# One weight part's home cleared of small router tiles, and a new order in the first units of mixer B

## The chip, the cores and the metric

The kernel runs on one core of one Trainium2 chip. The metric is the device time of one launch in microseconds, the median of several runs. All arrays are float32.

## What is computed

One layer of an encoder block over a sequence of 512 tokens of width 1024. Mixer B and the mixture of experts are the parts that matter here:

```python
def dilated_window_attention(q, k, v):            # mixer B: 12 heads in 3 groups (window, dilation)
    ...
            s = jnp.einsum('bqhd,bqkhd->bhqk', qb, kg).astype(jnp.float32)
            s = s - slopes[gi][:, None, None] * jnp.abs(jnp.asarray(off, jnp.float32))[None, None, :]
            s = jnp.where(valid[None, None], s, NEG_INF)
            lse = jax.nn.logsumexp(s, axis=-1)
            p = jnp.exp(s - lse[..., None]).astype(vg.dtype)
            outs.append(jnp.einsum('bhqk,bqkhd->bqhd', p, vg))
...
def expert_choice_swiglu(h, w_router, w_gate, w_up, w_down):
    aff = jax.nn.softmax(jnp.einsum('bsd,de->bse', h, w_router).astype(jnp.float32), axis=-1)
    g, idx = lax.top_k(jnp.swapaxes(aff, 1, 2), cap)          # 16 experts, 64 tokens each
    xin = jax.vmap(lambda hb, ib: hb[ib])(h, idx)
    a = jnp.einsum('becd,edf->becf', xin, w_gate)
    u = jnp.einsum('becd,edf->becf', xin, w_up)
    y = jnp.einsum('becf,efd->becd', jax.nn.silu(a) * u, w_down) * g[..., None].astype(h.dtype)
    ...
x = x + (gate_a * mixerA(h) @ w_o_a + gate_b * mixerB(h) @ w_o_b) @ w_out
x = x + expert_choice_swiglu(rms_norm(x, norm2_g), w_router, w_gate, w_up, w_down)
```

## The kernel before

Every engine has one program written out by hand, and semaphores tie the five together. Nothing is scheduled by a tool: what stands first in an engine's program is issued first, and an instruction that waits holds all that stands behind it on its engine.

The program has these stages: the projections of mixer A (from 0 us), the attention of mixer A in 32 units (`u` 0 to 31), mixer B, the gates and branch projections, the output projection (`res_steps`) with the router woven in, the selection of tokens, and then the experts in 8 pairs (`gate_up`, `down`, `scatter`).

**Mixer B.** Units 32 to 39 are the first half (`hp` 0, four token tiles for each of two heads) and 40 to 47 the second (`hp` 1). `NA` is 32. A unit goes round three engines:

- TensorE writes the scores (`scores_b`). It does so two units ahead: in unit `u` it issues the scores of `u + 2`, which must wait until VectorE has finished the maximum of unit `u` (`nmax_done`).
- VectorE adds the distances of the two dilated groups to a part of `dist` (line 2052), then makes biased scores and their maximum (line 2058, 768 columns).
- ScalarE takes the exponential (line 889), VectorE the reciprocal and the product with it (`norm_probs`, lines 1985 and 1987, semaphore `probs_normed`).
- TensorE transposes the result with six matmuls (`turn_probs`, lines 1352 and 1357), and ScalarE copies it out (`read_probs`).

The dilated distances are the same for every token tile, but the kernel overwrites the place in `dist` where they lie, so VectorE first copies them to `far` (line 2033).

Between these steps TensorE has projections to do that depend on nothing in mixer B: `fill` issues as many of their steps (three matmuls of 512 columns each, lines 1169 to 1171) as the plan `B_FILL` gives a unit. It is `([2, 3, 4, 5, 7, 8, 8, 8], [3, 6, 7, 8, 11, 14, 16, 16])`, counted up: two steps in unit 32, three in unit 40, and three in unit 41. The first fill of either half needs the output of the heads before to be read out of its PSUM bank (`low_o`, line 1991, semaphore `o_lo_done`).

**The expert weights.** They come in 192 parts of 1 MB, into 20 homes. SyncE issues all loads in the order of the parts, but for a few at the start. Until TensorE begins with the experts, 20 parts are loaded, each as soon as the tensors that used its home before are dead; each later part waits until TensorE has used the part that its home holds (`w_slot_used`). Part 17 goes to the second half of `wslot7`, 24 to 32 KB behind `W0`. Before, three small tiles of the router lay in that place (`w_rt_wide`, `four_parts`, `four_sum`), so SyncE waited for the third router result, `logits_done`, ahead of it:

```python
            load_part(15)
            sp.wait_ge(logits_done, 3)
            load_part(17)
            sp.wait_ge(sumsq2, 2)
            sp.wait_ge(x2_turned, 2)
            sp.wait_ge(xn_lo_done, 4)
            load_part(18)
            sp.wait_ge(proj_done, len(groups))
            for m in (7, 11, 12, 16):
                load_part(m)
```

**The squares of the second norm.** ScalarE squares each token tile for its sum (`square_x2`, line 1016); the squares themselves are thrown away, into `squares2`. GpSimd makes the reciprocal root of the sum, which VectorE needs for the logits. `high_xn` writes the high part of tile `c` to `xn`.

Of the kernel before, what the change touches and what calls it, by code (L numbers as in the profile page):

```python
# [28 lines left out]
ACT = mybir.ActivationFunctionType  # L29
# [5 lines left out]
P = 128  # L35
SEQ = 512
D = 1024
NT = SEQ // P
# [8 lines left out]
NE = 16  # L47
# [37 lines left out]
def encoder_block(nc, x, norm1_g, w_in, b_gates, q_norm_g, k_norm_g, w_o_a, w_o_b, w_out, norm2_g,  # L85
# [13 lines left out]
    def sb(name, shape, kib, dt=F32):  # L99
        return nc.alloc_sbuf_tensor_at(name, [P] + shape, dt, offset=base + int(kib * KIB))  # L100
# [48 lines left out]
    out_hi = sb("out_hi", [HALF_OUT, KC, P], W0, F32R)  # L149
    out_lo = sb("out_lo", [HALF_OUT, KC, P], W0 + 16, F32R)  # L150

    squares2 = sb("squares2", [D], 105.5)
    h2T = sb("h2T", [2, KC, P], 96)
    LANES = 32 + NE
    aff_wide = sb("aff_wide", [NT, 32], 111)
# [3 lines left out]
    slot_id = sb("slot_id", [CAP], 110)  # L159
    logit = sb("logit", [NT, NE], 110.25)  # L160
    w_rt = sb("w_rt", [KC, NE], 110.5)
    w_rt_wide = sb("w_rt_wide", [KC, 32], W0 + 28)
    four_parts = sb("four_parts", [2, P], W0 + 29)
    four_sum = sb("four_sum", [NE], W0 + 30)
    best = sb("best", [CAP], 101)
    left = sb("left", [2, SEQ // 2], 98)
    other = sb("other", [CAP], 100)
# [57 lines left out]
    with ExitStack() as ctx:  # L225
        def sem(name):
# [9 lines left out]

        turned_two = [psum[:, 4 + 2 * i:6 + 2 * i, :].rearrange("p b (k i) -> p (b k) i", i=P)
                      for i in range(2)]
        g1_wide = psum[:, 2:4, :].rearrange("p b n -> p (b n)")
        pp = bank[0:4]  # L240
        tp = bank[4:8]
# [167 lines left out]
        def tile_summed(eng, c, p=None):  # L409

            if p is None:
                p = 2 if c == NT - 1 else 1
            eng.wait_ge(proj_read_dve, N_COL + g_at[("res", p, c)] - RES0 + 1)
# [159 lines left out]
        def _(sp):  # L573
# [102 lines left out]
            load_part(13)  # L676
            load_part(14)
            load_part(15)
            sp.wait_ge(logits_done, 3)
            load_part(17)  # L680
            sp.wait_ge(sumsq2, 2)
            sp.wait_ge(x2_turned, 2)
# [91 lines left out]
        def _(act_):  # L774
# [236 lines left out]
            def square_x2(n, c, p, cols, into):  # L1011

                tile_summed(act_, c, p)
                if n:
                    act_.wait_ge(sumsq2, n)
                act_.activation(squares2[:, cols], x2[:, c, cols], ACT.Square, accum_out=into).then_inc(sumsq2, 1)

            def square_tile(c):
                square_x2(c, c, None, slice(0, D), ssq[:, c:c + 1])
# [21 lines left out]

            def high_xn(c):
                tile_summed(act_, c)
                act_.activation(xn_hi[:, c, :].rearrange("p (h k i) -> p h k i", h=2, k=HALF),
                                x2[:, c, :].rearrange("p (h i k) -> p h k i", h=2, k=HALF), ACT.Copy)\
                    .then_inc(xn_hi_done, 1)
# [118 lines left out]
        def _(pe):  # L1165
# [240 lines left out]
            for hp in range(2):  # L1406
                todo = [(g, at[g[1:]]) for g in col_groups[N_COL_A:N_COL_A + 1]] if hp == 0 else \
                    [(("gate", 0, 0), at[("ga", 0)]), (("gate", 0, 1), at[("gb", 0)])]
                first, end = NA + 2 * NT * hp, NA + 2 * NT * (hp + 1)
                first_behind = (col_groups[N_COL_A + 1], at[col_groups[N_COL_A + 1][1:]])  # L1410
                scores_b(first)
                if hp == 0:
                    values_a(OA - 1)
                    pe.wait_ge(proj_read_dve, N_COL_A)
                scores_b(first + 1)
                for u in range(first, end):
                    if u + 2 < end:
                        scores_b(u + 2)
                    if u == first:

                        pe.wait_ge(o_lo_done, OA + hp)
                    fill(B_FILL[hp], u - first, todo)
                    if u >= end - 2:
                        pe.wait_ge(nmax_done, end - 1)
                    if hp == 0 and u == end - 2:
                        col_steps(*first_behind, 0, 3)
                    if u == end - 1:
                        if hp == 0:
                            col_steps(*first_behind, 3, KC)
                        else:  # L1430
                            col_steps(("gate", 1, 0), at[("ga", 1)], 0, KC // 2)
                    turn_probs(u)
                pe.wait_ge(nmax_done, end)
                if hp == 0:
                    for g in col_groups[3 * NG:]:
                        col_group(g, at[g[1:]])

                    pe.wait_ge(proj_read_dve, 2 * NG + 2)
                    values_b(0)
                    pe.wait_ge(proj_read_dve, 4 * NG)  # L1440
                else:
                    col_steps(("gate", 1, 0), at[("ga", 1)], KC // 2, KC)
                    pe.wait_ge(proj_read_act, N_TOK + 2)
                    values_b(1)
                    col_group(("gate", 1, 1), at[("gb", 1)])
# [106 lines left out]
            pe.wait_ge(aff_done, 2)  # L1552
            turn_aff(0)

            keep_clock(4)
            pe.wait_ge(aff_done, NT)
            turn_aff(1).then_inc(route_turned, 1)

# [301 lines left out]
        def _(dve):  # L1860
# [169 lines left out]
                    low_o(O_LOW.index(u))  # L2030

            dve.wait_ge(dist_in, 16)
            settle(dve.tensor_copy(far[:, :], dist[:, 0, SEQ:SEQ + 2 * P]))
            for hp in range(2):
                first, end = NA + 2 * NT * hp, NA + 2 * NT * (hp + 1)
                if hp:
# [4 lines left out]
                for u in range(first, end + 2):  # L2041
# [4 lines left out]
                    if u < end:  # L2046
                        head, c = divmod(u - NA, NT)

                        dve.wait_ge(score_done, NA + 2 * (u - NA) + 1)
                        dve.tensor_tensor(dist[:, c, SEQ:SEQ + 2 * P],
                                          far_two[u % 2][:, 1, :, :].rearrange("p g n -> p (g n)"), far[:, :],
                                          ALU.add).then_inc(far_added, 1)
                        dve.wait_ge(far_added, u - NA + 1)
                        dve.wait_ge(score_done, NA + 2 * (u - NA) + 2)
# [396 lines left out]
```

## Time and profile before

| | us |
|---|---|
| median of 3 runs | 862.12 |
| lowest and highest | 861.91, 864.86 |
| the profiled execution | 861.86 |
| its span, first to last instruction | 859.8 |
| TensorE busy | 839.4 |
| VectorE busy | 379.3 |
| ScalarE busy | 264.1 |

The span is 2.06 us shorter than the time of the same execution; that is what lies around it. In the rows further down, PE is TensorE's matmuls, PEld its weight loads, DVE VectorE, ACT ScalarE, POOL GpSimd, and SPq the queue in which SyncE issues loads. A matmul's duration overlaps that of the next, so TensorE's pace is read from start to start.

### The profile page before, as it was taken

How to read it: one execution, taken by the hardware profiler on the slowest of the kernel's cores; microseconds unless marked ns; L12 is line 12 of the kernel's file. 1: busy time of each engine (PE TensorE's matmuls, PEld its weight loads, DVE VectorE, ACT ScalarE, POOL GpSimd, SP SyncE). 2: the span in 40 equal slices, each digit the busy share in tenths (PEclk: the TensorE clock that was granted, in tenths of full speed). 3: DMA queues.
4: the chain of work that ended last, by engine and by line, in shares of the span. 5: the costliest groups of instructions: out<-in, count | busy, mean ns of one | idle time of the engine just before them, and what ended most of it. 6: DMA issues, size and time to landing. Idle time of an engine off the chain costs nothing.

```text
span 859.8 us, 10399 instructions
## 1 busy us (share of the span) xinstructions
PE 839.4 (98%) x4197; PEld 513.2 (60%) x4197; DVE 379.3 (44%) x665; ACT 264.1 (31%) x461; POOL 29.0 (3%) x50
## 2 busy tenths in 40 slices
PE   9999999999999999999999999999999998989996
PEld 8898866687878888888534343344433433334343
DVE  6377987797715254427322237223131321321351
ACT  6333876695624233216011010010100101001231
POOL 1050000000000000003000000000000000000010
PEclk9999999999999999999999999999999999999999
DMA  9830112023034234884899999999999999999996
GB/s 285 179 98 2 50 50 98 25 76 109 20 123 143 84 107 144 311 356 180 331 410 425 429 428 426 429 428 427 428 428 427 426 430 428 426 423 429 427 420 265
DMA packets 81490, 239.19 MB, mean 278 GB/s; under 512 B 8102, under 2 KB 63526, under 8 KB 65828
## 3 DMA queue, kind: packets, MB, share of 16 engines
q1 hardware_dynamic: 76016, 235.94, 69.7%
q10 hardware_dynamic: 5284, 2.09, 1.0%
q8 instruction: 33, 0.54, 0.3%
q0 software_dynamic: 144, 0.51, 0.1%
q14 instruction: 13, 0.11, 0.0%
HBM read 235.92 MB, written 2.62 MB: 277 GB/s over the span
## 4 chain that ended last, share of the span: by engine, by line
PE 88%; DMA 8%; DVE 1%; ACT 1%; issue 1%; POOLq 0%; POOL 0%; SPq 0%; DVEq 0%; ACTq 0%
PE psum L1657 21%; PE psum L1169 11%; PE psum L1689 11%; PE psum L1171 11%; PE psum L1170 11%; DMA wslot<-in_w_down 7%; PE psum L1614 3%; PE psum L1708 3%; PE psum L1357 2%; PE psum L1818 2%; PE psum L1326 2%; PE psum L1369 1%; PE psum L1669 1%; PE psum L1175 1%; PE psum L1622 1%; PE psum L1379 1%
## 5 line engine op out<-in xcount | busy, mean ns | idle before, releaser
L1657 PE MATMUL psum<-wslot,xinT 128*64 128x512 f32 x1000 | 221.9, 595 | 3.7 <-DMA wslot<-in_w_up 1.9
L1657 PEld LDWEIGHTS psum<-wslot,xinT 128*64 128x64 f32 x1000 | 69.5, 137 | 141.3 <-issue 131.8
L1689 PE MATMUL psum<-wslot,actT 128*64 128x512 f32 x424 | 95.8, 596 | 4.5 <-DMA wslot<-in_w_down 4.5
L1169 PE MATMUL psum<-hT_hi,w_hi 128*128 128x512 f32 x208 | 82.4, 396 | 0.9 <-DVE oT_lo L1991 0.9
L1170 PE MATMUL psum<-hT_lo,w_hi 128*128 128x512 f32 x208 | 81.2, 390 | 0.0
L1171 PE MATMUL psum<-hT_hi,w_lo 128*128 128x512 f32 x208 | 81.2, 390 | 0.0
L1892 DVE TENSOR_TENSOR w_lo<-w_raw,w_hi 128x1024 fp32r<-128x1024 f32 (+1 forms) x46 | 52.9, 1174 | 44.4 <-ACT w_hi L805 44.3
L1689 PEld LDWEIGHTS psum<-wslot,actT 128*64 128x64 f32 x424 | 29.4, 137 | 60.4 <-issue 58.0
L1101 ACT ACTIVATE actT<-psum 128x512 f32<-128x512 f32 x16 | 9.6, 597 | 171.2 <-PE psum L1669 171.2
L2305 DVE TENSOR_TENSOR x<-x,psum 128x512 f32<-128x512 f32 x48 | 29.7, 681 | 57.0 <-PE psum L1708 57.0
L2295 DVE TENSOR_TENSOR y_lo<-psum,y_hi 64x512 fp32r<-64x512 f32 x28 | 19.3, 689 | 80.4 <-ACT y_hi L1111 80.0
L805 ACT ACTIVATE w_hi<-w_raw 128x1024 fp32r<-128x1024 f32 (+1 forms) x46 | 45.2, 1017 | 16.3 <-PE psum L1171 16.3
L1169 PEld LDWEIGHTS psum<-hT_hi,w_hi 128*128 128x128 f32 x208 | 39.0, 188 | 12.1 <-issue 2.8
L1171 PEld LDWEIGHTS psum<-hT_hi,w_lo 128*128 128x128 f32 x208 | 39.1, 188 | 8.4
L1170 PEld LDWEIGHTS psum<-hT_lo,w_hi 128*128 128x128 f32 x208 | 39.1, 188 | 7.8
L1096 ACT ACTIVATE act<-psum,slot_vals 128x512 f32<-128x512 f32 x16 | 11.0, 687 | 93.2 <-PE psum L1657 93.2
L2282 DVE SCALAR_TENSOR_TENSOR act<-psum,slot_vals,act 128x512 f32<-128x512 f32 x16 | 12.0, 750 | 59.1 <-ACT act L1096 59.0
L901 ACT ACTIVATE pT<-psum 128x512 f32<-128x512 f32 x48 | 28.5, 596 | 19.6 <-PE psum L1357 10.1
L1111 ACT ACTIVATE y_hi<-psum 64x512 fp32r<-64x512 f32 x28 | 16.5, 590 | 57.3 <-PE psum L1689 57.0
L1614 PE MATMUL psum<-xn,pick 128*128 128x512 f32 x120 | 29.4, 396 | 0.0
L2248 DVE TENSOR_TENSOR xinT<-psum,small 128x512 f32<-128x512 f32 x15 | 9.7, 686 | 40.0 <-PE psum L1622 40.0
L2288 DVE SCALAR_TENSOR_TENSOR act<-act,slot_fac,psum 128x512 f32<-128x512 f32 x16 | 12.0, 747 | 30.8 <-PE psum L1657 30.8
(285 smaller groups left out, 1306.5 us busy)
## 6 DMA issues: line engine op xcount, KB each, us to landing
wslot<-in_w_up SPq DMA_DIRECT2D x24, 2048.0 KB, 25.0
wslot<-in_w_gate SPq DMA_DIRECT2D x24, 2048.0 KB, 23.9
wslot<-in_w_down SPq DMA_DIRECT2D x22, 2048.0 KB, 22.4
w_raw<-in_w_in SPq DMA_DIRECT2D x34, 512.0 KB, 4.7
wslot<-in_w_up SPq DMA_DIRECT2D x15, 1024.0 KB, 11.0
wslot<-in_w_down SPq DMA_DIRECT2D x15, 1024.0 KB, 27.5
wslot<-in_w_gate SPq DMA_DIRECT2D x14, 1024.0 KB, 11.2
w_raw<-in_w_out SPq DMA_DIRECT2D x8, 512.0 KB, 4.9
```

The source lines that it names most:

```text
L805: act_.activation(hi, raw, ACT.Copy).then_inc(w_hi_done, 1)
L901: last = act_.activation(pT[:, head % 2, :, cols], tp[(0, 3)[u % 2]][:, :].rearrange("p (k i) -> p k i", i=P), ACT.Copy)
L1169: pe.matmul(out_, s_hi, m_hi, start=(k == 0), stop=False)
L1170: pe.matmul(out_, s_hi, m_lo, start=False, stop=False)
L1171: return pe.matmul(out_, s_lo, m_hi, start=False, stop=(k == n_k - 1))
L1614: mm = pe.matmul(bank[6 + f][:, :], pick[:, c, :, :], part[:, c, cols], start=(c == 0 and part is xn_hi), stop=(c == NT - 1 and part is xn ...
L1657: mm = pe.matmul(bank[2 * e + n][CAP * f:CAP * f + CAP, :], xinT[:, HALF * h + k, CAP * e:CAP * e + CAP], wslot[place_of(m)][:, k % PART, ...
L1689: mm = pe.matmul(bank[4 + e][CAP * f:CAP * f + CAP, :], actT[:, e, k, CAP * h:CAP * h + CAP], wslot[place_of(m)][:, k % PART, SEQ * f:SEQ ...
L1708: mm = pe.matmul(bank[added_bank(c, f)][:, :], give[:, p % 2, P * c:P * c + P], part[:, SEQ * f:SEQ * f + SEQ], start=(part is y_hi), stop ...
L1892: dve.tensor_tensor(lo, raw, hi.bitcast(F32), ALU.subtract).then_inc(w_split, 1)
L2295: dve.tensor_tensor(y_lo[rows, cols], bank[4 + e][CAP * f:CAP * f + CAP, :], y_hi[rows, cols].bitcast(F32), ALU.subtract).then_inc(y_lo_do ...
L2305: dve.tensor_tensor(part, part, bank[added_bank(c, f)][:, :], ALU.add).then_inc(added, 1)
```

## The change

1. `w_rt_wide`, `four_parts` and `four_sum` move to the 4 KB at 105.5 KB where `squares2` was. The squares of tiles 0 to 2 go to the place of tile `c` in `xn`, those of tile 3 to two PSUM banks (4 and 5). So `high_xn` waits for the squares of its tile, and the last squares wait for VectorE to have read tile 2 out of those banks. Four idle matmuls of `keep_clock` write to bank 1 instead of 5.
2. SyncE no longer waits for `logits_done` ahead of part 17.
3. In unit 32 VectorE adds the dilated distances from the last tile's place in `dist`, which is still whole until unit 35, and the copy to `far` comes in unit 33.
4. In the first unit of either half (32 and 40), TensorE's `turn_probs` stands ahead of the wait for `o_lo_done` and ahead of the fill.

```diff
-    squares2 = sb("squares2", [D], 105.5)
+    squares_by_tile = [sb(f"squares_by_tile{c}", [D], W0 + 64 + 8 * c) for c in range(NT - 1)]
-    w_rt_wide = sb("w_rt_wide", [KC, 32], W0 + 28)
-    four_parts = sb("four_parts", [2, P], W0 + 29)
-    four_sum = sb("four_sum", [NE], W0 + 30)
+    w_rt_wide = sb("w_rt_wide", [KC, 32], 105.5)
+    four_parts = sb("four_parts", [2, P], 106.5)
+    four_sum = sb("four_sum", [NE], 107.5)
+        last_squares = psum[:, 4:6, :].rearrange("p b n -> p (b n)")
             load_part(15)
-            sp.wait_ge(logits_done, 3)
             load_part(17)
-                act_.activation(squares2[:, cols], x2[:, c, cols], ACT.Square, accum_out=into).then_inc(sumsq2, 1)
+                if c < NT - 1:
+                    squares = squares_by_tile[c]
+                else:
+                    act_.wait_ge(h2T_dve_done, NT - 1)
+                    squares = last_squares
+                act_.activation(squares[:, cols], x2[:, c, cols], ACT.Square, accum_out=into).then_inc(sumsq2, 1)
             def high_xn(c):
                 tile_summed(act_, c)
+                act_.wait_ge(sumsq2, c + 1 + (c == NT - 1))
                     if u == first:
 
+                        turn_probs(u)
                         pe.wait_ge(o_lo_done, OA + hp)
                     fill(B_FILL[hp], u - first, todo)
...
-                    turn_probs(u)
+                    if u > first:
+                        turn_probs(u)
-            keep_clock(4)
+            keep_clock(4, bank[1])
             dve.wait_ge(dist_in, 16)
-            settle(dve.tensor_copy(far[:, :], dist[:, 0, SEQ:SEQ + 2 * P]))
+                        if u == NA + 1:
+                            settle(dve.tensor_copy(far[:, :], dist[:, NT - 1, SEQ:SEQ + 2 * P]))
                         dve.wait_ge(score_done, NA + 2 * (u - NA) + 1)
                         dve.tensor_tensor(dist[:, c, SEQ:SEQ + 2 * P],
-                                          far_two[u % 2][:, 1, :, :].rearrange("p g n -> p (g n)"), far[:, :],
+                                          far_two[u % 2][:, 1, :, :].rearrange("p g n -> p (g n)"),
+                                          dist[:, NT - 1, SEQ:SEQ + 2 * P] if u < NA + NT - 1 else far[:, :],
                                           ALU.add).then_inc(far_added, 1)
```

TensorE's order in unit 40, the first of the second half, before the change. The first rows are the scores of unit 42, then come three fill steps, the transposes of unit 40 (`probs_b_73`) and the scores of unit 43:

```order
L1338 MATMUL psum<-kB,oT_hi 128x2x128 [waits nmax_done]
L1338 MATMUL psum<-kB,qB 128x2x128
L1342 MATMUL psum<-kB,qB_next 128x512 x2
L1169 MATMUL psum<-hT_hi,w_hi 128x512 [waits proj_read_dve,w_split,o_lo_done]
L1170 MATMUL psum<-hT_lo,w_hi 128x512
L1171 MATMUL psum<-hT_hi,w_lo 128x512
...
L1352 MATMUL psum<-ident,probs_b_73 128x128 [waits pT_done,probs_normed]
L1352 MATMUL psum<-ident,probs_b_73 128x128
L1357 MATMUL psum<-ident,probs_b_73 128x128 x4
L1338 MATMUL psum<-kB,oT_hi 128x2x128 [waits nmax_done]
```

The same place in the changed kernel (its line numbers are 6 higher):

```order
L1344 MATMUL psum<-kB,oT_hi 128x2x128 [waits nmax_done]
L1344 MATMUL psum<-kB,qB 128x2x128
L1348 MATMUL psum<-kB,qB_next 128x512 x2
L1358 MATMUL psum<-ident,probs_b_73 128x128 [waits pT_done,probs_normed]
L1358 MATMUL psum<-ident,probs_b_73 128x128
L1363 MATMUL psum<-ident,probs_b_73 128x128 x4
L1175 MATMUL psum<-hT_hi,w_hi 128x512 [waits proj_read_dve,w_split,o_lo_done]
L1176 MATMUL psum<-hT_lo,w_hi 128x512
L1177 MATMUL psum<-hT_hi,w_lo 128x512
...
L1344 MATMUL psum<-kB,oT_hi 128x2x128 [waits nmax_done]
```

The six transposes with their wait for `probs_normed` moved ahead of nine fill matmuls in unit 40. In unit 32 they moved ahead of six in the same way.

## Rows read from the trace of the kernel before

**Rows 1.** The chain of work that ended last, shares of the span by engine.
```profile
PE 88%; DMA 8%; DVE 1%; ACT 1%; issue 1%; POOLq 0%; POOL 0%; SPq 0%; DVEq 0%; ACTq 0%
```

**Rows 2.** TensorE's waits (total, times, longest), and its last one in the timeline.
```profile
PE psum L1689 <- DMA wslot<-in_w_down: 4.5, 3, 1.9
...
774.58 7.09 PE L1689 MATMUL psum<-wslot,actT 128*64 128x512 f32 x32 [1.94 <-DMA wslot<-in_w_down]
```

**Rows 3.** Windows from 383.5 us on: busy times, granted clock, DMA share, GB/s.
```profile
383.50:397.50 14.00, 14.00 (x120) 11.94 (x118) 8.08 (x16) 11.95 (x18) 1.49 (x4) 1.00 0.02 7
...
416.60:420.60 4.00, 4.00 (x20) 1.37 (x22) 0.78 (x4) 0.00 (x0) 0.19 (x1) 1.00 0.38 84
420.00:440.00 20.00, 20.00 (x94) 7.47 (x92) 3.00 (x8) 2.57 (x3) 0.00 (x0) 1.00 0.99 373
440.00:690.00 250.00, 250.00 (x1185) 105.35 (x1183) 78.30 (x129) 29.40 (x49) 0.00 (x0) 1.00 1.01 427
690.00:850.00 160.00, 152.18 (x694) 64.39 (x690) 42.44 (x68) 24.66 (x39) 2.97 (x8) 1.00 1.01 425
```

**Rows 4.** SyncE's queue: three issues in its timeline, and its wait for the router.
```profile
371.13 0.91 SPq L632 DMA_DIRECT2D wslot<-in_w_up  x2
...
397.61 0.33 SPq L632 DMA_DIRECT2D wslot<-in_w_down  x1
...
418.48 8.93 SPq L632 DMA_DIRECT2D wslot<-in_w_down  x4
...
SPq L632 <- PE psum L1516: 25.6, 1, 25.6
```

**Rows 5.** Timeline of TensorE, units 40 and 41 of mixer B.
```profile
213.80 0.39 PE L1338 MATMUL psum<-kB,oT_hi 128*128 128x256 f32 x1 [0.45 <-DVE small L2058]
...
214.62 0.39 PE L1169 MATMUL psum<-hT_hi,w_hi 128*128 128x512 f32 x1
...
216.70 0.38 PE L1352 MATMUL psum<-ident,probs_b 128*128 128x128 f32 x2
...
217.27 0.36 PE L1338 MATMUL psum<-kB,oT_hi 128*128 128x256 f32 x1
```

**Rows 6.** Timeline of VectorE in the same units.
```profile
213.66 0.08 DVE L2058 DVE_READ_ACCUMULATOR2_ANT small<- 128x1 f32 x1
...
215.79 0.62 DVE L1987 TENSOR_SCALAR probs_b<-probs_b,small 128x768 f32<-128x768 f32 x1
```

**Rows 7.** Windows from unit 40 to the output projection.
```profile
214.40:231.00 16.60, 16.60 (x94) 14.06 (x93) 14.59 (x35) 11.69 (x26) 0.00 (x0) 1.00 0.11 33
231.00:381.00 150.00, 150.00 (x696) 122.55 (x695) 56.18 (x73) 47.30 (x64) 0.75 (x2) 1.00 0.51 174
```

**Rows 8.** Timeline of VectorE and TensorE, units 32 and 33.
```profile
165.70 0.29 DVE L2033 COPY far<-dist 128x256 f32<-128x256 f32 x1
...
166.03 0.42 DVE L2052 TENSOR_TENSOR dist<-psum,far 128x256 f32<-128x256 f32 x1
...
168.75 0.62 DVE L1987 TENSOR_SCALAR probs_b<-probs_b,small 128x768 f32<-128x768 f32 x1
169.28 0.68 DVE L1991 TENSOR_TENSOR oT_lo<-psum,oT_hi 128x512 fp32r<-128x512 f32 x1
...
170.02 0.51 PE L1169 MATMUL psum<-hT_hi,w_hi 128*128 128x512 f32 x1 [0.93 <-DVE oT_lo L1991]
...
172.74 0.62 DVE L1987 TENSOR_SCALAR probs_b<-probs_b,small 128x768 f32<-128x768 f32 x1
...
173.57 0.38 PE L1352 MATMUL psum<-ident,probs_b 128*128 128x128 f32 x2
```

**Rows 9.** Timeline around the last logits: ScalarE, GpSimd and VectorE.
```profile
399.24 0.42 ACT L1016 ACTIVATE squares<-x 128x256 f32<-128x256 f32 x1 [1.44 <-DVE x L2116]
...
400.44 0.55 POOL L719 TENSOR_TENSOR small<-small 128x1 f32<-128x1 f32 x1
...
401.10 0.29 DVE L2133 TENSOR_SCALAR logit<-psum,small 128x16 f32<-128x16 f32 x1
```

## The prediction, written before the changed kernel ran

> **What bounds the kernel now.** I began with the chain of work that ended last. TensorE holds 88% of it and DMA 8% [rows 1], so the question is which of the two sets the end. TensorE's waits answer it for the expert stage: only late there does it wait for weights, and the last of these waits ends at 774.58 us, after 1.94 us of idling [rows 2]. From there to the end the chain is TensorE's again.
>
> The windows of that stage show how it came to this. From 440 us on the loads run at 427 and 425 GB/s without a break [rows 3], and TensorE is a little faster than they are: it eats up the store of loaded parts until about 690 us and then waits. So the end is set by the moment at which the stream of loads becomes unbroken, plus its bytes at that rate. What sets that moment? Between 416.6 and 420.6 us the stream moves 84 GB/s, from 420 to 440 it moves 373 [rows 3]. All 20 homes are full there, and the next load goes out at 418.48 us [rows 4], when TensorE has used its first part. The stream therefore hangs on the moment when TensorE begins with the experts, and that on all that TensorE does before. The reader is to see a chain in two links: TensorE up to about 418 us, and a stream that TensorE itself starts.
>
> Ahead of the experts TensorE has almost no slack. From 214.4 to 231 us it is busy 16.60 of 16.60 us, and from 231 to 381 us 150.00 of 150 [rows 7]. A delay put in before that travels to the end whole.
>
> **Part 17 earlier: 0 us.** Before, its load leaves at 397.61 us, after a wait of 25.6 us for the router [rows 4]. After, it stands right behind part 15, whose issue is the second of the two at 371.13 us [rows 4], and it falls into a stretch in which the queues are idle (7 GB/s from 383.5 to 397.5 us, rows 3). One part is 1.049 MB, at 427 GB/s 2.46 us. But what is saved is not needed: the queue had already run dry by 416.6 us with this load in its old place, and the next home falls free only when TensorE has worked through a part. The 2.46 us become a longer pause ahead of 418.48 us. The parts read first have arrived in both kernels, since TensorE waits for none of them there: in all, its waits for loads come after 690 us. Bounds: 0, and a gain of 2.46 us if I misread the pause. I take 0.
>
> The Trainium skill (DMA: Bandwidth & Descriptors, section Where 436 GB/s comes from) gives 435 GB/s as the ceiling of the 16 engines together, and the 427 of the trace agree that the stream cannot be hurried. By that reading alone, a megabyte moved into an idle stretch would be worth its 2.4 us, an estimate from that page; it is rival 1 below.
>
> **Squares and router tiles: 0 us.** `high_xn` now waits for squares that stand ahead of it on ScalarE, so the wait is met. The wait of the last squares is for a copy that stands, in VectorE's program, ahead of the residual add for which these squares wait anyway. What no row shows is ScalarE writing squares to PSUM. The cover is thin in one place: the 256-column square starts at 399.24 us and takes 0.42, GpSimd's root runs from 400.44 for 0.55 to 400.99, and VectorE's step that needs it begins at 401.10 [rows 9]. So a square that is 0.1 us slower is hidden, and one that is 0.2 slower costs 0.1. I bound it by half and double the 0.42 us: it gains nothing (VectorE's own maximum stands just ahead of that step), or costs up to 0.3. The nearest row is the same instruction with its old target; 0 is my value.
>
> **The copy to `far`: 0 us by itself.** Its step is 0.33 us (165.70 to 166.03, rows 8). It leaves the way to the first exponential, so that the add, the maximum, the exponential and the product of unit 32 all come 0.33 us sooner: the product begins at 168.42 instead of 168.75, and `low_o` at 168.95 instead of 169.28. Then the copy stands in, ahead of the add of unit 33, and takes the 0.33 back. From unit 33 on VectorE is where it was.
>
> **Turning first in unit 32: a gain of 0.1 us.** Before, TensorE idles 0.93 us until `low_o` is done and starts its fill at 170.02 [rows 8]. After, it waits for the product instead: 168.42 + 0.62 = 169.04, plus some 0.06 us of signalling (the maximum's last piece ends at 213.74 and its waiter starts at 213.80, rows 5 and 6) = 169.10. Six transposes take 0.57 us (216.70 to 217.27, rows 5), so the fill starts near 169.7 instead of 170.02, and the scores of unit 35 some 0.7 us earlier than before. This lead is lost at once. The transposes of unit 33 need a product that ends at 172.74 + 0.62 = 173.36 [rows 8], and they started at 173.57 before; with the weight load behind the signal they can gain 0.0 to 0.15 us. VectorE is on its full pace from there to unit 36. I take 0.1.
>
> **Turning first in unit 40: a loss of 1.86 us.** Here nothing is sooner on VectorE: the copy was gone long before, and the order of the product and of `low_o` is unchanged. TensorE is free at 214.62 us, where it began its nine fill matmuls [rows 5]. Those nine (214.62 to 216.70, 2.08 us) were the work that hid the wait for the exponential and the product of unit 40. Now the transposes stand first, and they need the product that ends at 215.79 + 0.62 = 216.41 [rows 6]; with 0.06 us of signal and the short load it is 216.48. TensorE idles from 214.62 to 216.48. Then 0.57 us of transposes and 2.08 of fill, and the scores of unit 43 start at 219.13 instead of 217.27 [rows 5]: 1.86 us late.
>
> Who waits for it? VectorE's add of unit 43, the first that is late next, and VectorE has slack; behind TensorE there is the whole rest of the program, and TensorE has none [rows 7]. Could units 41 to 47 give some back? They would have to hold waits of TensorE that shrink, and 16.60 of 16.60 us busy says there is none. The lower bound is 1.79 us, from 214.62 to 216.41 with no signalling at all; the upper one is the 2.08 us of the whole fill.
>
> **Sum.** 0 + 0 + 0 − 0.1 + 1.86 = 1.76 us more. The profiled execution took 861.86 us, 0.26 less than the median of 862.12; with 1.76 they give 863.6 and 863.9. I put down **863.7**.
>
> **The rivals.**
>
> *1, the head start counts: 861.2 us.* If the stream were in truth unbroken from 398 us on, part 17 would take 2.46 us off the end, and 861.86 + 1.76 − 2.46 = 861.2. For it: the last 85 us hang on a load that lands at 774.58. Against it: 84 GB/s in the 4 us after 416.6 [rows 3]. Chance 0.08.
>
> *2, the waits of mixer B shrink behind unit 40: 861.9 us.* The loss is made good by units 41 to 47, or unit 32 gains as much as unit 40 loses. For it: TensorE and VectorE run at nearly the same pace there, and a busy share of 100% is modelled from pipelined matmuls. Against it: from 231 to 381 us, where no other engine is in step with TensorE, the same share is 150.00 of 150 [rows 7]. With half of the loss made good it is 862.8. Chance 0.14 for less than half the loss.
>
> *3, slower than before by more than can be mistaken: 868 us.* The new idling lets TensorE's clock fall from 2.4 to 1.2 GHz, and the work of units 40 and 41 behind it (some 4.5 us, 214.62 to 219.1) takes twice as long: 1.76 + 4.5 = 6.3. Against it is that a gap of 1.94 us before 774.58 stands in a window with granted clock 1.00 [rows 2, 3], and the new one is 1.86. It decides if idling of under 2 us is enough here and was not there. Chance 0.03.
>
> The Trainium skill (TensorE: Matmul & The Clock Gate, section Why this matters for your kernels) warns of idle gaps between bursts of matmuls for that reason. It is the rule that speaks against this change; the trace bears it out in no gap of this length.
>
> *The forecast* itself has 0.75, with its own range of 862.6 to 864.8.
>
> **How the numbers follow.** The forecast's range holds most; on the low side it must reach to rival 1, on the high side to a slower square (0.3), the 2.08 us bound, and the scatter of the median (one of three runs before was 864.86). That gives **861.0 to 865.3**. About 0.5%, or 4.3 us, is what a measurement of this kernel tells from no change. Below 857.8 no case ends (0.02 for what I have not seen), above 866.4 only rival 3 (0.03 and 0.01 for the unseen). So: faster 0.02, within 0.5% 0.94, slower 0.04.
>
> **What would show it.** In the profile of the changed kernel TensorE's first transposes of unit 40 carry a wait of about 1.8 us for the product on VectorE, and those of unit 32 one of 0.2 us in place of the 0.93. The first load that waits for TensorE's use of a part goes out near 420.2 us instead of 418.48. SyncE issues part 17 near 372 us, the rate between 412 and 418 us falls towards zero, and the last wait for a load ends near 776.3 instead of 774.58. The forecast is wrong if that load is not later, or if it is and the last wait ends where it did; the first would speak for rival 2, the second for rival 1.

## The result: 866.25 us against 863.22 before

The changed kernel took 866.25 us, the median of 10 runs (863.76 to 867.96). The kernel before, run beside it, had a median of 863.22 us in 10 runs (861.91 to 865.45). The ratio is 1.0035, with a 95% interval of 1.0023 to 1.0048: slower by a third of a per cent. The sign was forecast, the size was not. The difference is 3.03 us where 1.76 were forecast, and 866.25 us lies above the range.

The profiled execution spans 864.7 us, 4.9 more than the 859.8 of before. Three stretches hold the 4.9 us. The anchors are the first projection matmul (lines 1169 and 1175), which starts at 25.86 us before and 28.47 after, and the first expert matmul, at 416.51 and 421.01.

| stretch | before | after | difference |
|---|---|---|---|
| start to the first projection | 25.86 | 28.47 | +2.6 |
| first projection to the first expert matmul | 390.65 | 392.54 | +1.9 |
| first expert matmul to the end | 443.29 | 443.69 | +0.4 |

The chain of work that ended last is TensorE's as in rows 1:

```profile
PE 89%; DMA 7%; DVE 2%; issue 1%; ACT 1%; POOLq 0%; POOL 0%; DVEq 0%; ACTq 0%; SPq 0%
```

**The start.** TensorE's timeline of the changed kernel, with each row's start, duration, instructions and count:

```profile
5.60 3.78 PE L1297 MATMUL psum<-g_row,ones 1*128 1x512 f32 x4
9.31 1.65 PE L1181 MATMUL psum<-ident 128*128 128x128 f32 x6
10.75 1.91 PE L1192 MATMUL psum<-ident,x_in 128*128 128x128 f32 x8
```

The same rows of the kernel before:

```profile
5.60 2.18 PE L1291 MATMUL psum<-g_row,ones 1*128 1x512 f32 x4
7.71 0.94 PE L1175 MATMUL psum<-ident 128*128 128x128 f32 x6
8.48 1.04 PE L1186 MATMUL psum<-ident,x_in 128*128 128x128 f32 x8
```

The same instructions start at the same 5.60 us and run at about half the pace from there to about 13.5 us. The granted clock does not show it (a window of before, then of after: busy time of PE, PEld, DVE, ACT and POOL, granted clock, DMA share, GB/s). It is 1.00 in both, though 20 matmuls are counted in the one and 5 in the other:

```profile
8.00:10.00 2.00, 2.00 (x20) 2.00 (x19) 1.92 (x3) 1.32 (x3) 0.00 (x0) 1.00 1.03 401
8.00:10.00 2.00, 2.00 (x5) 0.69 (x4) 1.12 (x2) 1.13 (x2) 0.00 (x0) 1.00 1.02 398
```

The change touches nothing there. Of the kernels told below some started in the one way and some in the other, and the kernel before itself shows the two groups in its times: in its 35 runs of the first job 28 lie from 861.35 to 862.86 us and 7 from 864.32 to 866.17. So this is the lot of the single execution, worth some 2.5 us, and it takes 2.6 of the 4.9 us out of the comparison of the two traces. I call it a late start below.

**Mixer B, unit 40.** TensorE's wait for the products, after (total, times, longest):

```profile
PE psum L1358 <- DVE probs_b L1995: 2.1, 2, 1.7
```

Its timeline there:

```profile
216.71 0.63 PE L1348 MATMUL psum<-kB,qB_next 128*128 128x512 f32 x2
219.03 0.44 PE L1358 MATMUL psum<-ident,probs_b 128*128 128x128 f32 x2 [1.70 <-DVE probs_b L1995]
219.31 0.60 PE L1363 MATMUL psum<-ident,probs_b 128*128 128x128 f32 x4
219.66 0.47 PE L1175 MATMUL psum<-hT_hi,w_hi 128*128 128x512 f32 x1
...
221.83 0.28 PE L1344 MATMUL psum<-kB,oT_hi 128*128 128x256 f32 x1
```

The scores of unit 43 start at 221.83 − 28.47 = 193.36 us behind the first projection. Before it was 217.27 [rows 5] − 25.86 = 191.41. That is 1.95 us later. The busy time of TensorE from unit 40 on, which was 16.60 of 16.60 us [rows 7], has a hole of 16.60 − 14.90 = 1.70 us, the wait itself (windows):

```profile
217.30:233.90 16.60, 14.90 (x86) 12.70 (x86) 12.90 (x30) 10.42 (x24) 0.00 (x0) 1.00 0.05 13
233.90:383.90 150.00, 150.00 (x695) 122.51 (x695) 57.72 (x77) 48.26 (x67) 0.75 (x2) 1.00 0.51 172
```

**Unit 32.** The other wait in the total is 2.1 − 1.7 = 0.4 us. TensorE's timeline, which answers to rows 8:

```profile
171.74 0.44 PE L1358 MATMUL psum<-ident,probs_b 128*128 128x128 f32 x2
172.01 0.60 PE L1363 MATMUL psum<-ident,probs_b 128*128 128x128 f32 x4
172.37 0.48 PE L1175 MATMUL psum<-hT_hi,w_hi 128*128 128x512 f32 x1
```

The fill of unit 32 starts at 172.37 − 28.47 = 143.90 us behind the first projection, where it was 170.02 − 25.86 = 144.16 [rows 8]: 0.26 us sooner.

**Squares.** The 256-column square with its target in PSUM takes 0.39 us, after 0.42 [rows 9] (timeline of ScalarE):

```profile
403.74 0.39 ACT L1021 ACTIVATE psum<-x 128x256 f32<-128x256 f32 x1 [1.45 <-DVE x L2126]
```

**Loads.** SyncE's queue in the timeline:

```profile
376.58 0.43 SPq L633 DMA_DIRECT2D wslot<-in_w_down  x1
401.70 0.33 SPq L633 DMA_DIRECT2D wslot_once<-in_w_down  x1
...
422.98 0.33 SPq L633 DMA_DIRECT2D wslot<-in_w_down  x1
```

Its longest wait:

```profile
SPq L683 <- DVE xn L2158: 24.6, 1, 24.6
```

The windows:

```profile
386.10:400.10 14.00, 14.00 (x116) 11.73 (x114) 7.56 (x15) 11.18 (x16) 1.50 (x4) 1.00 0.33 135
416.60:420.60 4.00, 3.28 (x26) 2.95 (x25) 1.90 (x8) 0.38 (x1) 0.00 (x0) 1.00 0.55 229
417.01:421.01 4.00, 2.91 (x23) 2.57 (x23) 2.04 (x8) 0.71 (x2) 0.00 (x0) 1.00 0.44 184
421.10:425.10 4.00, 4.00 (x20) 1.37 (x22) 0.78 (x4) 0.00 (x0) 0.20 (x1) 1.00 0.29 55
440.00:690.00 250.00, 250.00 (x1185) 104.60 (x1182) 75.24 (x124) 29.41 (x49) 0.00 (x0) 1.00 1.01 427
690.00:850.00 160.00, 152.27 (x689) 63.48 (x691) 45.52 (x73) 24.07 (x38) 2.98 (x8) 1.00 1.01 425
```

The four microseconds before the first expert matmul, in the kernel before:

```profile
412.51:416.51 4.00, 2.91 (x24) 2.57 (x23) 2.04 (x8) 0.72 (x2) 0.00 (x0) 1.00 1.00 418
```

Part 17 leaves at 376.58 us instead of behind the router, and part 18 has inherited the long wait (24.6 us on line 683, for 25.6 on line 632 in rows 4). The first load that waits for TensorE leaves at 422.98 us, 1.97 us behind the first expert matmul; before it was 418.48 [rows 4] − 416.51 = 1.97. The rates from 440 us on are those of rows 3. The last wait for a load:

```profile
779.41 2.80 PE L1697 MATMUL psum<-wslot,actT 128*64 128x512 f32 x12 [1.35 <-DMA wslot<-in_w_down]
```

It is 4.83 us later than in rows 2; the start gives 2.6, mixer B 1.9, and 0.3 come behind the first expert matmul.

### The profile page after: what moved, and what is told of

It reads as the page before. It is cut to its first block, busy times and chain, and to the rows that moved or that the text cites. A ratio compares the mean times of both kernels' runs of the same rounds, so it can differ in the third digit from the quotient of the medians.

```text
span 864.7 us, 10404 instructions
## 1 busy us (share of the span) xinstructions
PE 843.5 (98%) x4197; PEld 514.9 (60%) x4197; DVE 379.5 (44%) x665; ACT 264.4 (31%) x461; POOL 29.1 (3%) x50
## 4 chain that ended last, share of the span: by engine, by line
PE 89%; DMA 7%; DVE 2%; issue 1%; ACT 1%; POOLq 0%; POOL 0%; DVEq 0%; ACTq 0%; SPq 0%
PE psum L1665 21%; PE psum L1175 11%; PE psum L1697 11%; PE psum L1177 11%; PE psum L1176 11%; DMA wslot<-in_w_down 7%; PE psum L1622 3%; PE psum L1716 3%; PE psum L1363 2%; PE psum L1826 2%; PE psum L1332 2%; PE psum L1375 1%; PE psum L1181 1%; PE psum L1677 1%; PE psum L1630 1%; PE psum L1385 1%
```

## The experiments

The theory to begin with: unit 40's order costs 1.9 us and TensorE hands them on to the end; all else costs nothing, and what exceeds it in the median is scatter. The rivals: another part of the change costs the rest, or the new idling does, by a fall of TensorE's clock.

The same anchors for all kernels, one profiled execution each, in us. "Quarter point" is the value under which a quarter of a kernel's runs lie, less that of the kernel before in the same job; where late starts are the minority, they move it less than the median. "Low clock" counts runs with a mean granted clock of TensorE under 0.995.

| kernel | median | ratio, 95% | quarter point | projection to experts | experts to end | low clock |
|---|---|---|---|---|---|---|
| before, first of three jobs | 862.24 | | | 390.65 | 443.29 | 0 of 35 |
| after | 866.25 | 1.0035 (1.0023 to 1.0048) | +3.6 | 392.54 | 443.69 | 4 of 10 |
| 1 unit 32, tiles, part 17 | 862.61 | 1.0006 (0.9993 to 1.0019) | +0.3 | 390.52 | 443.76 | 0 of 12 |
| 2 unit 40 alone | 865.19 | 1.0032 (1.002 to 1.0044) | +1.9 | 392.66 | 443.00 | 4 of 12 |
| 3 tiles and part 17 | 862.57 | 1.0005 (0.9992 to 1.0019) | 0.0 | 390.70 | 443.92 | 0 of 12 |
| 4 unit 32 alone | 862.58 | 1.0002 (0.999 to 1.0014) | +0.2 | 390.56 | 443.21 | 0 of 12 |
| 5 unit 40, idling filled | 865.39 | 1.0035 (1.0024 to 1.0046) | +2.3 | 392.61 | 443.90 | 0 of 12 |
| 6 unit 40, longer idling | 867.42 | 1.006 (1.0045 to 1.0076) | +4.8 | 394.89 | 444.37 | 3 of 6 |
| 7 tiles alone | 862.23 | 0.9996 (0.9984 to 1.0008) | 0.0 | 390.67 | 443.31 | 0 of 12 |
| 8 unit 40, one step first | 863.75 | 1.0023 (1.0012 to 1.0034) | +1.4 | 391.90 | 443.26 | 0 of 12 |
| 9 start edited, before | 863.27 | 1.0013 (0.9998 to 1.0029) | +0.6 | 390.63 | 443.52 | 0 of 12 |
| 10 start edited, after | 865.81 | 1.0037 (1.0021 to 1.0053) | +2.6 | 393.90 | 443.46 | 0 of 12 |
| 11 start edited, after, filled | 865.85 | 1.0039 (1.0024 to 1.0055) | +2.4 | 392.50 | 443.59 | 0 of 12 |

The first four ran together, then four, then three; the kernel before had medians of 862.24, 862.28 and 862.64 us in these jobs. The changed kernel had run earlier, beside ten runs of before of which five, from 864.18 us up, stand where late starts stand. Of its own ten runs only the lowest stands near the price of the order alone (863.76 − 861.91 = 1.85 us between the two lowest); four have a low clock, and the other five lie 2.5 us and more above it.

**1: the changed kernel with unit 40 as before.**

```
@@ mixer B, unit `first`
-                        turn_probs(u)
+                        if hp == 0:
+                            turn_probs(u)
...
-                    if u > first:
+                    if u > first or hp:
                         turn_probs(u)
```

> The changed kernel, but turn_probs stands ahead of the fill only in unit 32, no longer in unit 40. Theory A (the one part of the change that costs is the order in unit 40, 1.9 us; the rest of the 3.0 us between the medians is the start of the program, which takes 2.4 to 2.6 us longer in some executions of either kernel): the experts begin within 0.1 us of where they began before, counted from the first projection; time 0.0 to 0.2 us under the kernel before in equal starts, and the transposes of unit 40 carry no wait. Theory B (the moved tiles and the early part 17 cost some 1.1 us on their own, in the expert stage or at the start): 1.0 to 1.2 us over the kernel before. Theory C (the order in unit 32 costs too): some 0.3 us or more over it by the first score of the second half.

Measured: no difference from before that can be told, and the loss between projection and experts is gone (390.52 against 390.65).

**2: the kernel before with unit 40's order alone.**

```
@@ mixer B, unit `first`, in the kernel before
+                        if hp:
+                            turn_probs(u)
                         pe.wait_ge(o_lo_done, OA + hp)
...
-                    turn_probs(u)
+                    if u > first or not hp:
+                        turn_probs(u)
```

> The kernel before with one edit: turn_probs ahead of the wait and the fill in unit 40 alone. Theory A: a wait of 1.7 us at the transposes of unit 40, the scores of unit 43 1.9 us later, the experts 1.9 us later counted from the first projection, and all of it in the time: 1.8 to 2.0 us over the kernel before in equal starts. Theory B: 1.9 us here too, but then 1.1 us short of the changed kernel. The rival of the prediction that units 41 to 47 give it back: under 1 us.

Measured: ratio 1.0032, nearly all of the change's 1.0035. Between projection and experts it loses 2.0 us. These two edits of a few lines settle which part of the change is at work.

**3: the changed kernel with mixer B as before,** so that only the tiles, the squares and the early part 17 are left. **4: the kernel before with the far copy moved and unit 32's order alone.**

```
@@ 4: VectorE
-            settle(dve.tensor_copy(far[:, :], dist[:, 0, SEQ:SEQ + 2 * P]))
...
+                        if u == NA + 1:
+                            settle(dve.tensor_copy(far[:, :], dist[:, NT - 1, SEQ:SEQ + 2 * P]))
@@ 4: TensorE
+                        if hp == 0:
+                            turn_probs(u)
...
-                    turn_probs(u)
+                    if u > first or hp:
+                        turn_probs(u)
```

> The changed kernel with mixer B as it was before: only the moved tiles, the squares in xn and PSUM, and part 17 issued behind part 15. Theory A: no change (within 0.2 us in equal starts); part 17 leaves near 372 us, and the stream of loads pauses longer ahead of the first load that waits for TensorE. Theory B: 1.1 us slower than before. The rival that the head start counts: 2.4 us faster.

> The kernel before with the edits of unit 32 alone: the copy to far one unit later, and turn_probs ahead of the fill there. Theory A: the scores of unit 42 come 0.0 to 0.1 us earlier counted from the first projection, and the time does not change by more than that in equal starts. Theory C: they come later by 0.3 us or more.

Measured: 1.0005 and 1.0002, both without a difference. The gain of unit 32 shows in the traces alone: 390.56 against 390.65, and 390.52 against the 390.70 of the third kernel, so 0.1 to 0.2 us.

One thing stood out in the single runs. In the changed kernel and in the second, 8 of 22 had a mean granted clock of 0.993 or 0.994. In the other kernels of this job, before among them, no run of 71 was under 0.995. So the next job asked for the clock.

**5: the idling of unit 40 filled.** The second kernel, with seven matmuls in the pause whose result nobody reads:

```
                         if hp:
+                            pe.wait_ge(pT_done, u)
+                            keep_clock(7, tp[3])
                             turn_probs(u)
```

> The kernel before with unit 40's transposes first, as in the second experiment, and with seven matmuls of the identity by itself (about 0.25 us each, into a free bank; nobody reads them) in the 1.7 us in which TensorE would wait for the product. The order of the work stays, and so does its loss of 1.9 us; only the idling goes. Theory A, that the median's surplus over 1.9 us and the single runs with a mean granted clock of 0.993 to 0.994 come from the idling: no run of this kernel is under 0.995, and the median is 864.1 to 864.4. Theory B, that they have to do with the late work and not with the idling, or with the day's chip: runs under 0.995 stay at about 4 in 12, and the median stays near 865.2.

Measured: by the clock theory A is right, 0 of 12 runs under 0.995. (Its partner with the pause left open, kernel 2, ran in the job before; in the fifth kernel's own job the open pause was there only in the longer form of kernel 6, with 3 of 6.) By the median it is wrong: 865.39 us, not 864.1 to 864.4. Filling the pause took the low clocks away and gave the median nothing back. Its runs fall in groups: five lie from 863.6 to 864.57, and five from 866.22 up. The latter stand 2.6 us and more over the lowest, where late starts stand in the kernel before.

**6: a longer pause.** Unit 40's transposes stand ahead even of the scores of unit 42:

```
+                    if u == first and hp:
+                        turn_probs(u)
                     if u + 2 < end:
                         scores_b(u + 2)
```

> The kernel before with unit 40's transposes ahead even of the scores of unit 42. TensorE is then free from 213.3 us and idles until 216.4, 3.1 us instead of 0.45 and 1.7, and the scores of unit 42 start 3.3 us late. By the order alone: VectorE is held up as well, and the experts begin 3 to 3.5 us late, median 865.3 to 865.8. Theory A (idling lets the clock fall in some executions): the longer pause does it in at least as many runs as the 1.7 us one (4 to 8 in 12 with a mean clock under 0.995), and the median goes to 866.5 to 868. Theory B: no more than 4 in 12, median under 866.

Measured: 3 of 6 runs under 0.995, median 867.42, as A said, and the profiled execution was one with the fall. TensorE's timeline of this kernel, and below it two windows:

```profile
216.69 0.69 PE L1352 MATMUL psum<-ident,probs_b 128*128 128x128 f32 x2 [3.12 <-DVE probs_b L1990]
217.17 1.06 PE L1357 MATMUL psum<-ident,probs_b 128*128 128x128 f32 x4
```

```profile
210.00:215.00 5.00, 3.57 (x42) 2.82 (x38) 4.31 (x8) 1.64 (x4) 0.00 (x0) 1.00 0.35 103
215.00:220.00 5.00, 3.31 (x12) 3.03 (x13) 2.38 (x6) 1.93 (x5) 0.00 (x0) 0.66 0.01 2
```

The granted clock is 0.66 in the mean from 215 to 220 us, and 1.00 before and behind. Four transposes take 1.06 us for the 0.60 of the changed kernel's trace.

**7: the tiles alone,** the third kernel with part 17 waiting for the router again.

```
             load_part(15)
+            sp.wait_ge(logits_done, 3)
             load_part(17)
```

> The tiles, the squares and their waits as after the change, but mixer B as before and part 17 again behind the wait for the router's logits. Theory A, that the early part 17 costs the 0.5 us that the stretch from the first expert matmul to the end is longer in all three kernels that have it: the stretch is back to 443.0 to 443.3 us. Theory B, that the moved tiles and squares cost them: it stays at 443.7 to 443.9. Median 862.2 by A, 862.6 by B, which the medians alone can hardly tell apart.

Measured: 443.31 us from the experts to the end, as A expected, and a ratio of 0.9996. The tiles and squares cost nothing. But A itself, that the early part 17 costs the 0.5 us, doesn't hold as said: kernels 5 and 6, which have part 17 in its old place, took 443.90 and 444.37 us. In all of the traces of before, after and the first eight experiments the loads from the first expert matmul on leave at the same distances from it, to 0.02 us (1.97, 12.29, 16.41, 21.56 us and so on); so the moment of issue is not what differs. The stretch scatters by 0.5 us and more from one kernel's trace to another's, and whether part 17 adds to it can't be told from one trace each.

**8: a shorter pause.** One of the three fill steps stands ahead of the transposes, two behind:

```
-                    fill(B_FILL[hp], u - first, todo)
+                    if u == first and hp:
+                        fill([1], 0, todo)
+                        turn_probs(u)
+                        fill([3], 0, todo, 1)
+                    else:
+                        fill(B_FILL[hp], u - first, todo)
```

> The kernel before with unit 40's transposes behind the first of its three fill steps, the other two behind them. One step is 0.69 us, so the idling is 1.7 - 0.7 = 1.0 us, and by the count of uncovered time the experts begin 1.2 us late instead of 1.9: median near 863.5. If the clock falls in some runs at 1.7 us of idling, a pause of 1.0 us shows whether a shorter one does it less: theory A expects 0 to 2 runs in 12 under 0.995, theory B about as many as with 1.7 us.

TensorE's timeline of this kernel:

```profile
214.62 0.40 PE L1169 MATMUL psum<-hT_hi,w_hi 128*128 128x512 f32 x1
...
216.48 0.44 PE L1352 MATMUL psum<-ident,probs_b 128*128 128x128 f32 x2 [0.99 <-DVE probs_b L1993]
```

Measured: a pause of 0.99 us, the experts 391.90 − 390.65 = 1.25 us late, 1.4 at the quarter point, and no run under 0.995. The loss follows the uncovered time, step by step: 0, 1.25 and 2.0 us for three, one and no fill steps ahead (kernels before, 8 and 2).

**9, 10 and 11: the start.** To take the late starts out of the comparison I put three matmuls of ones (`full_rows`) between the two that spread g1 and took out three idle matmuls (`keep_clock`) behind them, in the kernel before (9), in the changed kernel (10), and in the changed kernel with the pause filled (11):

```
                 pe.matmul(bank[2 + f][:, :], ones[0:1, :], g1_row[0:1, SEQ * f:SEQ * f + SEQ],
                           start=True, stop=True).then_inc(g1_spread, 1)
+                if f == 0:
+                    full_rows(3)
             pe.wait_ge(ident_in, 16)
-
-            keep_clock(3, bank[1])
```

> The kernel before with one edit at the very start: three of the matmuls that only keep TensorE busy are moved between the two that spread g1 (these have a single row of weights, and in the executions that begin slowly all that follows them up to 13.5 us runs at half pace, 2.6 us late at the first projection). In the traces so far the start is of this kind in three of ten. If the long stretch of single-row matmuls lets it happen, the runs near 864.5 go away and 12 runs lie within 861.3 to 863.3, median 862.2. If the start is decided otherwise, some 2 to 4 runs in 12 stay at 864.3 to 866 and the median is the same.

> The changed kernel with the same edit at the start. Its median was 3.0 us over that of before, where the traces show 1.9 us for unit 40. Theory C, that the rest is the lot of the single execution (late starts, which 5 or 6 of its 10 runs seem to have had against 1 in 5 of before, and the clock in unit 40): with a steady start the median is 1.9 us over that of the kernel before with the steady start, plus 0.2 to 0.5 for runs with the fallen clock, so 864.2 to 864.8. If the edit doesn't steady the start, another 12 runs still tell: theory C expects late runs in 2 to 4 of 12 and a median of 864.2 to 865. Theory D, that something else in the change costs 1 us in every run: 865.2 to 865.8 again, and no run under 864.5.

> The changed kernel with the same edit at the start and with seven matmuls that nobody reads in the pause of unit 40, as in the fifth experiment. The clock then has no pause to fall in: no run with a mean clock under 0.995, where the kernel without them has 2 to 5 in 12. The order's 1.9 us stay. By theory C the median is 863.9 to 864.4, by theory D 865 or more.

Measured: the edit failed at its aim. Late starts stay (9 has three runs from 866.03 to 867.95 us), and the quarter point is 0.6 us worse. The medians that theory C named are missed: 865.81 and 865.85 us. Against kernel 9, which has the same start, 10 is 2.54 us slower in the median and 2.0 at the quarter point, and 11 is 2.58 and 1.8 slower; C's own terms, 1.9 and 0.2 to 0.5, come to 2.1 to 2.4 for kernel 10. Its forecast of the clock, two to five low means of 12 with the pause open, is missed too: 10 has none, like 11. But theory D, 1 us more in every run, falls too: 10 has 863.62, 863.90 and 864.38 us, and 11 has five runs from 864.20 to 864.80. The profiled execution of 10 shows, in the order of the change itself, what the clock does there. TensorE's timeline, and below it a window:

```profile
216.81 0.69 PE L1361 MATMUL psum<-ident,probs_b 128*128 128x128 f32 x2 [1.69 <-DVE probs_b L1998]
217.29 1.06 PE L1366 MATMUL psum<-ident,probs_b 128*128 128x128 f32 x4
218.01 0.78 PE L1175 MATMUL psum<-hT_hi,w_hi 128*128 128x512 f32 x1
...
220.99 0.28 PE L1347 MATMUL psum<-kB,oT_hi 128*128 128x256 f32 x1
```

```profile
215.00:220.00 5.00, 3.31 (x12) 2.83 (x12) 3.68 (x10) 2.73 (x7) 0.00 (x0) 0.66 0.03 8
```

The same rows of 11, where the pause is filled:

```profile
214.90 1.72 PE L1181 MATMUL psum<-ident 128*128 128x128 f32 x14
216.76 0.44 PE L1361 MATMUL psum<-ident,probs_b 128*128 128x128 f32 x2
217.04 0.60 PE L1366 MATMUL psum<-ident,probs_b 128*128 128x128 f32 x4
217.40 0.48 PE L1175 MATMUL psum<-hT_hi,w_hi 128*128 128x512 f32 x1
...
219.53 0.28 PE L1347 MATMUL psum<-kB,oT_hi 128*128 128x256 f32 x1
```

From the first transpose to the scores of unit 43 it is 4.18 us in the one and 2.77 in the other, and the experts begin 393.90 − 392.50 = 1.4 us later. After a pause of 1.69 us TensorE ran for a while at the lower of its two levels, 1.2 GHz (0.66 is the mean of the five microseconds), and it cost 1.4 us. The mean of this run's clock is 0.995, so the count under 0.995 in the table misses some of the falls, and zero of 12 for kernel 11 says little, since kernel 10 has zero as well. Nor is a low mean proof of this fall: in the third job one of 29 runs of the kernel before had 0.994.

## Why the prediction was right in sign and wrong in size

**Unit 40 held.** The term was 1.86 us. The traces give 1.95 us at the scores of unit 43; at the experts they give 1.9 for the changed kernel, in which unit 32's gain is counted, and 2.0 for kernel 2, which has none. The wait's row says 1.70 us, not 1.86, since it counts from the end of the last score matmul (216.71 + 0.63 = 217.34), which in the trace of before overlaps the next one by 0.16 us (214.14 + 0.64 = 214.78, against a start at 214.62). Behind the pause the first matmuls are a little slower (the first of the fill 0.47 us for 0.39). Experiments 1, 2 and 8 show cause and size. Rival 2, that units 41 to 47 give it back, falls with them: the loss at unit 43 is the loss at the experts.

**Unit 32, the far copy, tiles and squares held.** A gain of 0.1 us was forecast and 0.1 to 0.2 seen; the wait is 0.4 us, not 0.2. Kernels 3 and 7 show the rest at nothing that can be measured.

**Part 17 held.** Rival 1 is out. The megabyte moved ahead became a pause: the four microseconds before the first expert matmul carry 418 GB/s in the trace of before and 184 in that of after, and the first gated load keeps its 1.97 us behind that matmul. Less the late start's 2.61 us, that load leaves at 420.4 us (420.2 forecast), and the last wait for a load ends at 776.8 (776.3 forecast).

**Two steps failed.** The first is the dismissal of the third rival. I gave it 0.03, since a gap of 1.94 us stands before 774.58 in a window with granted clock 1.00, and wrote: "It decides if idling of under 2 us is enough here and was not there". It is enough, in some executions and not in others: the trace of 10 has the fall behind 1.69 us of idling and those of after and 2 have none behind 1.70 and 1.69, and 8 of 22 runs of the changed kernel and the second have the low mean that points to it. One gap in one trace without a fall was evidence that a fall isn't certain, and I read it as evidence that it doesn't come. The price was wrong as well: not 4.5 us for all the work of two units at half pace, but 1.4. In hindsight, a chance near a third at 1.4 us is a term of some 0.5 us in the sum (an estimate from these counts), not a case at its edge. The Trainium skill (TensorE: Matmul & The Clock Gate, section Why this matters for your kernels) asks to avoid gaps between bursts of matmuls. The gap that it still lets pass is longer than this one of 1.69 us, so by that section the change was safe, and not spoken against as the prediction has it. In the trace of 10 the clock fell behind this gap, and the measurement decides.

The second is the base. That a range must reach to "the scatter of the median (one of three runs before was 864.86)" stood in the working as a detail of the range. That run was one of a group: late starts, 2.5 us. In the job that timed the change, five of the ten runs of the kernel before were at 864.18 us and over, and its median 863.22, not 862.12. So of the 2.55 us between forecast and result 1.10 are the kernel before's own median, and 1.45 are more loss than was forecast: 3.03 us less the 1.58 that lie between 862.12 and 863.7.

**How the 1.45 us divide is only partly shown.** The clock's part is shown for one execution of this order (1.4 us, kernel 10). The single runs of kernel 2 agree: the four with a low mean span 863.2 to 864.7 us, six of the other eight 861.4 to 862.3, and without the four its median is 864.16 us, 1.92 over that of before.

But kernels 5 and 11, in which the pause is filled, have medians just as high. At the quarter point kernel 5 is 0.4 us over the order's 1.9; kernel 11's 2.4 holds the 0.6 of the edited start, and against kernel 9 it is 1.8. What lifts the two medians beyond that are ten of 24 runs that stand 2.5 us and more over their kernel's lowest. In the changed kernel's profiled execution, and in those of 4 and 7, such a run was a late start. The kernel before has 7 of 35, 6 of 29 and 6 of 29 of them in the three jobs, and kernel 9 has 3 of 12. The mean granted clock points the same way in kernel 11: four of its five such runs have a mean of 0.998 or more and none of its other seven has, as in the kernel before 17 of 19 and 11 of 74. In kernel 5 it doesn't separate them. Nothing that the change touches runs before 13.5 us, so I take the surplus of late starts in the kernels with unit 40's order for chance. Set against the 19 of 93 of before, ten or more of 24 would come by chance about once in 30 times (an estimate from these counts). So this is argued, not shown, and stays open. A smaller scatter lies outside the spans: most runs are 2.0 us longer than their span, but a few (one of ten of the changed kernel, three of 29 of before in the third job) are some 3.0 to 3.3 us longer.

## What to carry to other kernels

Work that stands between a producer's result and its consumer on an in-order engine is a cover: before putting the consumer first, take the time at which its input is ready less the time at which the engine comes free. Here that gave 1.86 us, and 1.9 to 2.0 were measured. Where the prediction opens a new gap on TensorE, however short, price the clock as a case with a real chance. And look at all single runs for groups before a difference of a few tenths of a per cent is forecast or judged: a median of three can lie in either group.

## What the hardware did that I had not expected

- A pause of 1.69 us on TensorE, after one of 0.46, was followed by a stretch at the lower clock in one trace and not in the traces of after and 2. With the pause filled by idle matmuls (kernel 5) or cut to 0.99 us (kernel 8) no mean under 0.995 was seen in 24 runs.
- At the start the same instructions took half the pace up to 13.5 us in the traces of after, 4 and 7, the full pace from 5.6 us on in those of before, 1, 2 and 5 (the others rose early and fell back for a while, with little loss). The granted clock is shown as 1.00 in both, so there the pace must be read from the durations: 3.78 us and 2.18 for the same four matmuls.
- With the loads issued at the same distances from the first expert matmul, the stretch from it to the end still scattered from 443.00 to 444.37 us.
